# Feed-forward up projection computed with stationary weights and moving tokens, on one Trainium2 core

## What is computed

```python
x = x + merged @ w_out                       # (256, 2048)
h2 = rms_norm(x, norm_ffn_g)                 # x * rsqrt(mean(x*x) + eps) * g
u = square(relu(h2 @ w_up))                  # w_up (2048, 8192)
x = x + u @ w_down                           # w_down (8192, 2048)
return rms_norm(x, norm_final_g)
```

## Time and profile before

| | |
|---|---|
| median of 3 runs | 1581.27 us |
| the profiled execution | 1582.0 us |
| its span (first to last instruction) | 1580.2 us |
| mean granted clock of TensorE | 0.998 of full speed |
| TensorE busy with matmuls | 1565.5 us, 99%, 6988 matmuls |
| VectorE busy | 1028.0 us, 65% |
| ScalarE busy | 792.0 us, 50% |
| HBM read | 298.55 MB, 190 GB/s over the span |

### The profile page before, as it was taken

How to read it: one execution, slowest core, us unless ns; L and a number is a source line. 1 busy time by engine, 2 the same in 40 slices (tenths; PEclk the granted TensorE clock), 3 DMA queues, 4 the chain that set the end, 5 groups by cost and what they waited for, 6 DMA issues and landing times.

```text
span 1580.2 us, 18921 instructions
## 1 busy us (share of the span) xinstructions
PE 1565.5 (99%) x6988; PEld 1291.2 (82%) x6988; DVE 1028.0 (65%) x1335; ACT 792.0 (50%) x1013; POOL 36.9 (2%) x48
## 2 busy tenths in 40 slices
PE   8999999999999999999999999999999999999997
PEld 7888888888888888888878888888888888878886
DVE  6877876454556777666699877337753576337744
ACT  5555555434444454444444555555554555545553
POOL 0000000000000000000000000000000000000000
PEclk9999999999999999999999999999999999999999
DMA  9645444566655565556565877888778887888873
GB/s 365 200 134 172 159 151 157 187 193 202 228 172 175 186 211 162 187 188 210 199 217 190 252 243 232 253 232 255 236 239 247 239 252 215 249 239 240 255 217 113
DMA packets 154072, 333.93 MB, mean 211 GB/s; under 512 B 5280, under 2 KB 5408, under 8 KB 149536
## 3 DMA queue, kind: packets, MB, share of 16 engines
q1 hardware_dynamic: 149120, 299.65, 56.1%
q0 software_dynamic: 4464, 32.51, 10.8%
q10 hardware_dynamic: 432, 1.02, 0.2%
HBM read 298.55 MB, written 2.10 MB: 190 GB/s over the span
## 4 chain that ended last, share of the span: by engine, by line
PE 94%; DVE 2%; DMA 1%; issue 1%; ACT 1%; SPq 0%; POOLq 0%; POOL 0%; DVEq 0%; ACTq 0%
PE acc L402 91%; PE sps L414 1%; DVE buf L943 1%; PE pps L432 1%; DMA low<-raw 1%; DMA raw<-in_w_in 1%; PE pps L425 0%; DVE wlo L934 0%; ACT whi L623 0%; DVE ta_lo L1335 0%; PE tps L467 0%; PE tps L534 0%; PE tps L533 0%; PE tps L535 0%; DVE final L1347 0%
## 5 line engine op out<-in xcount | busy, mean ns | idle before, releaser
L623 ACT ACTIVATE whi<-raw 128x1024 fp32r<-128x1024 f32 x543 | 573.3, 1059 | 673.1 <-PE acc L402 669.6
L934 DVE TENSOR_TENSOR wlo<-raw,whi 128x1024 fp32r<-128x1024 f32 x481 | 586.9, 1224 | 486.7 <-ACT whi L623 483.7
L402 PE MATMUL acc<-whi,ta_hi 128*128 128x512 f32 x1308 | 517.0, 395 | 4.5 <-DVE ta_lo L1004 2.3
L402 PE MATMUL acc<-whi,ta_lo 128*128 128x512 f32 x1308 | 509.6, 390 | 0.0
L402 PE MATMUL acc<-wlo,ta_hi 128*128 128x512 f32 x1180 | 459.4, 389 | 0.0
L402 PEld LDWEIGHTS acc<-whi,ta_hi 128*128 128x128 f32 x1308 | 245.7, 188 | 58.9 <-issue 4.1
L402 PEld LDWEIGHTS acc<-whi,ta_lo 128*128 128x128 f32 x1308 | 245.5, 188 | 51.7
L402 PE MATMUL acc<-whi,tb_hi 128*128 128x512 f32 x736 | 287.2, 390 | 0.0
L402 PE MATMUL acc<-whi,tb_lo 128*128 128x512 f32 x736 | 286.4, 389 | 0.0
L402 PEld LDWEIGHTS acc<-wlo,ta_hi 128*128 128x128 f32 x1180 | 221.7, 188 | 47.3 <-issue 2.4
L402 PE MATMUL acc<-wlo,tb_hi 128*128 128x512 f32 x616 | 239.7, 389 | 0.0
(11 more groups left out here) (136 smaller groups left out, 807.7 us busy)
## 6 DMA issues: line engine op xcount, KB each, us to landing
raw<-in_w_in SPq DMA_DIRECT2D x67, 1024.0 KB, 5.3
raw<-in_w_up SPq DMA_DIRECT2D x64, 1024.0 KB, 5.4
raw<-in_w_down SPq DMA_DIRECT2D x64, 1024.0 KB, 5.2
raw<-in_w_gate SPq DMA_DIRECT2D x32, 1024.0 KB, 5.3
low<-raw POOLq DMA_DIRECT2D x31, 1024.0 KB, 8.1
raw<-in_w_att SPq DMA_DIRECT2D x16, 1024.0 KB, 5.0
raw<-in_w_ret SPq DMA_DIRECT2D x16, 1024.0 KB, 5.0
raw<-in_w_out SPq DMA_DIRECT2D x16, 1024.0 KB, 5.3
```

The source lines that it names most:

```text
L402: last = nc.tensor.matmul(acc[B.parity][:, t, :], a[:, k, tok], b, start=(k == 0 and n == 0), stop=(k == KCH - 1 and n == 2))
L623: nc.scalar.activation(whi[:, s:s + UCH, :], raw[:, u * UCH:(u + 1) * UCH, :], ACT.Copy).then_inc(hi_ready, 1)
L934: V_.tensor_tensor(wlo[:, s:s + UCH, :], raw[:, u * UCH:(u + 1) * UCH, :], whi[:, s:s + UCH, :].bitcast(f32), ALU.subtract).then_inc(lo_re ...
```

## The change

Three things change in the feed-forward part.

- The 16 up blocks go through `gemm_turned`. For each chunk and each of the 4 groups of 128 weight columns (`GCH`), the weights are the stationary operand and all 256 tokens the moving one. A chunk has 12 matmuls with 256 moving columns in place of 6 with 512. The output lies with the up columns on partitions and tokens along them; `acc_t` is a view of the same accumulator as 4 groups x 256 tokens, two groups in each bank.
- The relu is one instruction without a scale (`relu_turned`), the square is unchanged, and `tb_hi` and `tb_lo` are made from `buf[0]` itself (`hi_from_squared`, `lo_from_squared`), between units 5 and 6 of the next block. The 16 transposes per up block are gone.
- The square of rstd2 (`ms2_inv`) is applied where a down block is added to the residual (`add_down`, two instructions of 512 elements with a scalar per token in place of one of 1024), and in the last block's two adds.

Behind the last block's matmuls, 16 more into the unused bank `sps` are issued: 5 with 512 moving columns, 5 that move the same two columns again and again (512 in all), 6 with 128.

```diff
--- before.py
+++ after.py
@@ -181,6 +181,7 @@
+        ms2_inv = place("ms2_inv", [P, 2], f32)
...
+        acc_t = [a[:].rearrange("p t n -> p (t n)").rearrange("p (m n) -> p m n", n=S) for a in acc]
...
+        squared = buf[0][:].rearrange("p t (m n) -> p (t m) n", n=S)
...
+            def gemm_turned(B, hi, lo, u0, u1):
+
+                for u in range(u0, u1):
+                    if u == 0:
+                        pe.wait_ge(evacuated[B.parity], B.turn)
+                    by_dma = u >= DVE_UNITS
+                    if by_dma:
+                        pe.wait_ge(low_full, B.before * 16 + 32)
+                        pe.wait_ge(hi_ready, B.part(u))
+                    else:
+                        pe.wait_ge(lo_ready, B.low(u))
+                    for kk in range(UCH):
+                        k, slot = u * UCH + kk, (u * UCH + kk) % (KCH // 2)
+                        low = low4[:, k - DVE_UNITS * UCH, :] if by_dma else wlo[:, slot, :]
+                        for m in range(GCH):
+                            col = slice(m * P, (m + 1) * P)
+                            for n, (w, a) in enumerate(((whi[:, slot, :], hi), (whi[:, slot, :], lo), (low, hi))):
+                                last = nc.tensor.matmul(acc_t[B.parity][:, m, :], w[:, col], a[:, k, :],
+                                                        start=(k == 0 and n == 0 and m % 2 == 0),
+                                                        stop=(k == KCH - 1 and n == 2), skip_group_check=True)
                     last.then_inc(unit_done, 1)
...
@@ -569,19 +594,17 @@
                 B = [Block(B6 + i, 8, q) for i in range(8)]
                 if first:
                     pe.wait_ge(h2T_ready, 3)
-                    gemm(B[0], ta_hi, ta_lo, 0, 6)
+                    gemm_turned(B[0], ta_hi, ta_lo, 0, 6)
                     pe.wait_ge(h2T_ready, 4)
-                    gemm(B[0], ta_hi, ta_lo, 6, 8)
+                    gemm_turned(B[0], ta_hi, ta_lo, 6, 8)
                 else:
-                    gemm(B[0], ta_hi, ta_lo, 0, 8)
-                for i in range(1, 5):
-                    hi, lo = (ta_hi, ta_lo) if i < 4 else (tb_hi, tb_lo)
-                    if i == 4:
-                        pe.wait_ge(t_free, q * 4 + (T_STAGE6 + 3))
-                    gemm(B[i], hi, lo, 0, 6)
-                    if i == 4:
-                        pe.wait_ge(t_free, q * 4 + (T_STAGE6 + 4))
-                    gemm(B[i], hi, lo, 6, 8)
+                    gemm_turned(B[0], ta_hi, ta_lo, 0, 8)
+                for i in range(1, 4):
+                    gemm_turned(B[i], ta_hi, ta_lo, 0, 8)
+                pe.wait_ge(t_free, q * 4 + (T_STAGE6 + 3))
+                gemm(B[4], tb_hi, tb_lo, 0, 6)
+                pe.wait_ge(t_free, q * 4 + (T_STAGE6 + 4))
+                gemm(B[4], tb_hi, tb_lo, 6, 8)
                 for i in range(5, 8):
                     if i == 7 and last:
                         gemm_by_tile(Block(LAST))
@@ -603,6 +626,14 @@
                                 done = nc.tensor.matmul(acc[B.parity][:, t, :], a[:, k, tok], b,
                                                         start=(k == 0 and n == 0), stop=(k == KCH - 1 and n == 2))
                     done.then_inc(tile_done, 1)
+                spare_bank = sps[:].rearrange(flat)
+                for _ in range(5):
+                    nc.tensor.matmul(spare_bank, tb_hi[:, 0, 0:P], whi[:, 0, :], start=True, stop=True)
+                for _ in range(5):
+                    nc.tensor.matmul(spare_bank.rearrange("p (a b) -> p a b", b=2), tb_hi[:, 0, 0:P],
+                                     whi[:, 0, 0:2].unsqueeze(1).to_broadcast([P, COLS // 2, 2]), start=True, stop=True)
+                for k in range(6):
+                    nc.tensor.matmul(spare_bank[:, 0:P], tb_hi[:, k, 0:P], whi[:, 0, 0:P], start=True, stop=True)
...
                     split(B[0], 5, 8)
                 for i in range(1, 5):
                     split(B[i], 0, 4)
-                    if first and i == 1:
-                        act.wait_ge(rstd2_ready, 1)
-                    else:
-                        act.wait_ge(t_full, q * 4 + (T_STAGE6 + i - 1))
-                    scaled_relu(B[i - 1])
+                    relu_turned(B[i - 1], q * 4 + (12 + i - 1))
                     negated(B[i])
-                    split(B[i], 4, 8)
-                    hi_from_turned(q * 4 + (T_STAGE6 + i - 1), tb_hi, i - 1)
+                    split(B[i], 4, 6)
+                    hi_from_squared(q * 4 + i, tb_hi, i - 1)
+                    split(B[i], 6, 8)
                 for i in range(5, 8):
                     if i == 7 and last:
                         split_last(B[i])
@@ -900,8 +928,14 @@
                         act.wait_ge(unit_done, B.unit(u - 4))
                     nc.scalar.activation(last_slot(0, u), raw[:, u * UCH:(u + 1) * UCH, :], ACT.Copy).then_inc(hi_ready, 1)
 
-            def scaled_relu(B):
-                scaled(B, buf[0], ACT.Relu, rstd2).then_inc(evacuated[B.parity], 1)
+            def relu_turned(B, freed):
+                act.wait_ge(unit_done, B.unit(UNITS - 1))
+                act.wait_ge(t_free, freed)
+                nc.scalar.activation(squared, acc_t[B.parity], ACT.Relu).then_inc(evacuated[B.parity], 1)
+
+            def hi_from_squared(n, dst, g):
+                act.wait_ge(u_ready, n)
+                nc.scalar.activation(dst[:, g * GCH:(g + 1) * GCH, :], squared, ACT.Copy).then_inc(t_hi, 1)
...
                 dve.wait_ge(evacuated[B.parity], B.turn + 1)
                 V_.tensor_tensor(buf[0][:], buf[0][:], buf[0][:], ALU.mult).then_inc(u_ready, 1)
 
+            def lo_from_squared(n, hi, lo, g):
+                dve.wait_ge(t_hi, n)
+                V_.tensor_tensor(lo[:, g * GCH:(g + 1) * GCH, :], squared, hi[:, g * GCH:(g + 1) * GCH, :].bitcast(f32),
+                                 ALU.subtract).then_inc(t_free, 1)
+
+            def add_down(B, j):
+                dve.wait_ge(unit_done, B.unit(UNITS - 1))
+                for t in range(TILES):
+                    sl = mix[:, t, j * COLS:(j + 1) * COLS]
+                    last = V_.scalar_tensor_tensor(sl, acc[B.parity][:, t, :], ms2_inv[:, t:t + 1], sl, ALU.mult, ALU.add)
+                last.then_inc(evacuated[B.parity], 1)
+
             def stage6(q, first, last=False):
                 B = [Block(B6 + i, 8, q) for i in range(8)]
                 if not first:
                     split(B[0], 0, 4)
-                    add_residual(Block(B6 - 1, 8, q), 3)
+                    add_down(Block(B6 - 1, 8, q), 3)
                     split(B[0], 4, 8)
                 for i in range(1, 5):
                     split(B[i], 0, 4)
                     square(B[i - 1])
-                    split_and_turn(B[i], 4, 8, q * 4 + (T_STAGE6 + i - 1), buf[0][:], u_ready, q * 4 + i)
-                    lo_from_turned(q * 4 + (12 + i), tb_hi, tb_lo, i - 1)
+                    split(B[i], 4, 6)
+                    lo_from_squared(q * 4 + (12 + i), tb_hi, tb_lo, i - 1)
+                    split(B[i], 6, 8)
+                if first:
+                    dve.wait_ge(rstd2_ready, 1)
+                    mine.step(V_.tensor_tensor(ms2_inv[:], rstd2[:], rstd2[:], ALU.mult))
+                    mine.wait(dve)
                 for i in range(5, 8):
...
-                    add_residual(B[i - 1], i - 5)
+                    add_down(B[i - 1], i - 5)
...
             for t in range(TILES):
                 sl = mix[:, t, early:D]
                 dve.wait_ge(tile_done, t + 1)
-                V_.tensor_tensor(sl, sl, acc[0][:, t, :], ALU.add).then_inc(added, 1)
+                V_.scalar_tensor_tensor(sl, acc[0][:, t, :], ms2_inv[:, t:t + 1], sl, ALU.mult, ALU.add).then_inc(added, 1)
```

More of the change, by code:

```diff
@@ L403, in gemm @@
                                                         start=(k == 0 and n == 0), stop=(k == KCH - 1 and n == 2))
+                    last.then_inc(unit_done, 1)
+            def gemm_turned(B, hi, lo, u0, u1):
[17 more added lines that the diff above has]
+                                                        stop=(k == KCH - 1 and n == 2), skip_group_check=True)
                     last.then_inc(unit_done, 1)
```

## The result

The changed kernel takes **1602.26 us** (median of 4 runs, 1601.75 to 1602.80) against 1581.15 for the kernel before (4 runs on the same chip): 21.1 us slower, ratio 1.0134, 95% interval 1.0121 to 1.0147. Forecast was 1600.3.

The account below looks back on a forecast made before the run. TensorE was taken as the bound, paying per step between matmuls. 1582.0 + 20.6 for added matmuls - 0.6 - 1.0 for stalls gave 1601.0, or 1600.3 us as median; range 1578 to 1612.

Parts of the forecast that it names:

- What bounds the kernel: Whole kernel: TensorE busy 1565.5 of 1580.2 us is the bound; work taken off VectorE counts only where TensorE waits for it.
- Twice as many, half as wide: Up blocks: 1536 more matmuls of 256 columns, priced from -13.3 to +69.6 us, with +20.6 us taken.
- (c): Up-block matmuls: 13.4 ns goes with each matmul and its load, 120.1 ns a step, +20.6 us; chance 0.57.
- By the column: Rival for up-block matmuls: the overhead goes with the columns, 113.3 ns a step, no change, 1580 us; chance 0.19.
- the lower price: Rival for up-block matmuls: halves cost less than half, 109 ns a step, -13.3 us, 1566 us; chance 0.10.
- the upper: Upper end for up-block matmuls: bytes read set the step, 136 ns, +69.6 us, 1649 us; half of a 0.14 chance.
- load and stream side by side: Reason given for the 13.4 ns: each weight load runs beside the preceding matmul's columns, something that happens once per load.
- The load no longer covered: Rival in up blocks: a 0.11 us load outlasts 0.107 us of columns; 1608 us, or 1649; chance 0.14.
- The stalls: TensorE's waits in first up blocks: -0.6 us at 890.48, -1.0 us at 1414.02 in the last turn, from longer cover.
- Down adds: Down blocks: one add becomes two with a scalar, 1.38 us for 1.21, +0.17 us 15 times, covered, so 0.
- ScalarE, end: One relu in place of two and a moved hi part cost 0; sixteen final matmuls end before the output DMAs, 0.

Follow-up runs that it names:

- after_wide: The changed kernel with the up blocks' matmuls as before, 6 with 512 columns per chunk, output not the reference's: 1581.26 us against 1581.21, ratio 1.0001.
- b16_after: The changed kernel with hi and lo parts in 2 bytes, all lo parts made by VectorE, no sixteen matmuls at the end: 1513.49 us, ratio 0.9571.

## Why the prediction was right

- **What bounds the kernel**: right. Taking 112 us off VectorE moved nothing (`after_wide`, 1.0001).
- **Twice as many, half as wide**: value (c) was right, 120.0 ns a step; +20.5 us where +20.6 was forecast, in the turned form and in the plain one. By the column (113.3), the lower price (109) and the upper (136) fell with the same row. The reason I gave, load and stream side by side, is not borne out: beside 512 columns the cost does not shrink with the stationary operand, and it belongs to the type. No row before had told (c) from the others, so that this value came true is in part luck. The lower bound came from another type (and the eight of the earlier trace rows are transposes by TensorE), and another type (2 bytes) does pay what that bound said.
- **The load no longer covered**: not at 256 columns; the floor is 110 ns, below 120. At 192 and 128 columns it sets the step.
- **The stalls**: the step that failed. -0.6 for the earlier trace rows came true. -1.0 for the earlier trace rows did not: the extra microsecond of cover was there, but of the first up blocks of turns 1 to 3 two had a DMA that landed over 10 us after its issue (10.2 and 10.3) instead of one (10.1), which left 0.62 and 0.67 us; why they land later was not tested. And the loop's jump back brought 1.30 us that no row of before showed. Forecast -1.6, measured +0.7; these 2.3 us account for the distance of 2.0 from 1600.3 to 1602.26.
- **Down adds**: 1.40 us a pair, +0.19 for the forecast +0.17, and the cover held in the down blocks of the changed kernel. **ScalarE, end**: as forecast; the sixteen matmuls ran beside the last tile's output.

## What to carry to other kernels

Where TensorE is busy all the time, count its instructions, not only its columns: find the step between starts, take off columns over the clock, and the rest is paid per matmul. Here it is 13.3 ns with 4-byte reduced operands and about 2.5 ns with 2-byte ones, so 512 columns are worth keeping in the first case, and a layout that halves them is nearly free in the second. Work taken from an engine that nobody waits for pays only once something else has made that engine the bound.

## What the runs showed that was not expected

- Beside 512 moving columns a load a quarter as wide saves nothing (231 ns against 226.7), beside 256 it saves some 4 ns (115 against 119). 16 moving columns repeated step 242 ns, slower than 512 different ones at 226.7.
- A loop body of 1152 matmuls is fetched again on its second pass, one of 768 is not. The fetch cost a wait of 1.3 us in the changed kernel and none in `b16_after`, where it began earlier.
- Behind a gap of 1.65 us and 2 us of 128-column matmuls the clock fell to 1.2 GHz (a gap of 1.67 us ahead of 256-column ones left it at 2.4), and the rest of 1536 matmuls of 128 columns in a row did not bring it back in 328 us, though they fill TensorE's time.
